# Orders of work on VectorE, ScalarE and the load queue in a two-block fp32 network, changed in six places

## What is computed

```python
h = rms_norm(x, norm1_g);  p = h @ w_in                       # 1024 -> 3328
uv = gelu(p[..., :1024]);  s_in = p[..., 1024:1280]
gates = sigmoid(p[..., 1280:] + b_gate)                        # g_a, g_b
br_a = gmlp_spatial_gating(uv[..., :512], uv[..., 512:], ...)  # layer norm of v, per group w_s @ v, times u
br_b = s5_mixer(s_in, ...)                                     # complex scan in both directions, gelu, y * sigmoid(y @ w_glu)
x = x + (g_a * (br_a @ w_up_a) + g_b * (br_b @ w_up_b)) @ w_out
x = x + expert_choice_ffn(rms_norm(x, norm2_g), ...)           # softmax, top 64 of 512 for each of 16 experts
x = rms_norm(x, final_g)
# second block
u = rms_norm_2(x);  x_lru, g_lru, q, k, v, g_ret = split(u @ w_in_2)
mixed = concat(rms_norm_2(rg_lru(conv(x_lru)) * gelu(g_lru)), group_norm(retention(q, k, v)) * silu(g_ret))
h = x + mixed @ w_out_2
up = conv(rms_norm_2(h) @ ffn_up_w);  a, v = split(up)
return rms_norm_2(h + (gelu(a) * v) @ ffn_down_w)
```

## Time and profile before

| | us |
|---|---|
| median of 3 runs (lowest to highest) | 1932.91 (1932.58 to 1933.05) |
| profiled execution, own time | 1933.91 |
| its span, first to last instruction | 1932.1 |
| PE busy | 1750.1 (91%) |
| DVE busy | 667.9 (35%) |
| ACT busy | 443.6 (23%) |

### The profile page before, as it was taken

The page is one execution under the profiler, slowest core; times in us unless marked ns, Lnnn a source line. Parts: engine busy times, 40 slices in busy tenths (PEclk is TensorE's granted clock), DMA queues, the critical chain, the costliest instruction groups (busy, mean ns, idle before and its releaser), DMA issues. The chain is left out here.

```text
span 1932.1 us, 19429 instructions
## 1 busy us (share of the span) xinstructions
PE 1750.1 (91%) x8120; PEld 1045.2 (54%) x8120; DVE 667.9 (35%) x903; ACT 443.6 (23%) x546; POOL 0.2 (0%) x4
## 2 busy tenths in 40 slices
PE   5998997899998898988979889789999999999997
PEld 4877774434342332423324233247767778888885
DVE  6865463201011010100101001047735466555644
ACT  4433322101010000100001010055433343323332
POOL 0000000000000000000000000000000000000000
PEclk9999999899999999999999999999999999999999
DMA  4313644699999999999999999950412213232311
GB/s 160 99 48 107 218 136 184 261 428 428 427 428 429 429 428 429 428 429 428 428 428 429 428 428 428 428 220 28 153 44 88 87 66 109 87 109 87 109 44 44
DMA packets 76389, 492.47 MB, mean 255 GB/s; under 512 B 7472, under 2 KB 12592, under 8 KB 51504
## 3 DMA queue, kind: packets, MB, share of 16 engines
q1 hardware_dynamic: 76336, 491.71, 63.1%
HBM read 487.49 MB, written 2.10 MB: 253 GB/s over the span
## 5 line engine op out<-in xcount | busy, mean ns | idle before, releaser
L1166 PE MATMUL ps<-xs,xe 128*64 128x512 f32 x2048 | 462.9, 600 | 65.8 <-DMA xs<-w_up 33.2
L1166 PEld LDWEIGHTS ps<-xs,xe 128*64 128x64 f32 x2048 | 142.1, 137 | 379.2 <-issue 265.9
L1178 PE MATMUL ps<-xs,hidT 128*64 128x512 f32 x1024 | 229.7, 596 | 13.6 <-DMA xs<-w_down 8.9
L412 DVE TENSOR_TENSOR lo<-raw,hi 128x2048 fp32r<-128x2048 f32 (+1 forms) x73 | 164.9, 2259 | 217.7 <-ACT hi L403 210.6
L1394 DVE TENSOR_TENSOR hid<-hid,ps 128x512 f32<-128x512 f32 x32 | 20.6, 684 | 524.3 <-PE ps L1166 524.3
L403 ACT ACTIVATE hi<-raw 128x2048 fp32r<-128x2048 f32 (+1 forms) x73 | 137.9, 1889 | 232.0 <-PE ps L466 96.9
L466 PE MATMUL ps<-xh,hi 128*128 128x512 f32 x416 | 167.8, 403 | 10.3 <-DVE ga L921 5.8
L466 PE MATMUL ps<-xl,hi 128*128 128x512 f32 x416 | 164.3, 395 | 0.0
L442 PE MATMUL ps<-xh,hi 128*128 128x512 f32 x384 | 151.4, 394 | 4.3 <-ACT hi L403 3.2
L1178 PEld LDWEIGHTS ps<-xs,hidT 128*64 128x64 f32 x1024 | 74.0, 137 | 147.6 <-issue 127.7
L442 PE MATMUL ps<-xl,hi 128*128 128x512 f32 x384 | 150.2, 391 | 0.0
(11 more groups left out here) (415 smaller groups left out, 1783.6 us busy)
## 6 DMA issues: line engine op xcount, KB each, us to landing
xs<-w_up SPq DMA_DIRECT2D x64, 2048.0 KB, 32.8
xs<-w_gate SPq DMA_DIRECT2D x64, 2048.0 KB, 31.9
xs<-w_down SPq DMA_DIRECT2D x64, 2048.0 KB, 31.3
raw<-w_in SPq DMA_DIRECT2D x25, 1024.0 KB, 7.2
raw<-ffn_up_w SPq DMA_DIRECT2D x24, 1024.0 KB, 5.1
raw<-ffn_down_w SPq DMA_DIRECT2D x12, 1024.0 KB, 5.1
raw<-w_out SPq DMA_DIRECT2D x8, 1024.0 KB, 5.1
xin<-x_t SPq DMA_DIRECT2D x4, 512.0 KB, 7.4
```

Source lines behind the costliest of these rows:

```text
L412: dve.tensor_tensor(lo[slot][:, 0:size], raw[:, raw_slot(n), 0:size], hi[slot][:, 0:size].bitcast(F32), ALU.subtract).then_inc(sem("lo_don ...
L1166: mm = pe.matmul(ps[64 * half:64 * half + 64, bank + b, :], xe[:, k, CAP * u:CAP * (u + 1)], xs[n % NXS][:, f:f + 512], start=(k == 0), st ...
L1178: mm = pe.matmul(ps[64 * nn:64 * nn + 64, YB, :], hidT[:, 4 * (c % 2) + kk, CAP * half:CAP * (half + 1)], xs[n % NXS][:, kk * D + nn * 512 ...
```

## The change

The number of matmuls, activations, vector instructions and DMAs stays; they come in another order. `prm` gets a semaphore of its own, `prm_in`. `x` and chunk 0 are issued right behind it. ACT's Exp and Sin stand before `xh`; hi and lo of chunk 0 stand in the middle of the 8 tiles. lo of 6 and the layer norm stand before `WT`, lo of 7 behind `hs_ready`. Chunk 9 is loaded before the 32 `INT` DMAs. `z` is computed for banks 2, 3, 0, 1, and only the last two wait for `yblk`. The gated unit stands behind the first quarter of chunk 12's hi part. The merges and the lo of 14 to 17 alternate. hi of 20 comes before `take_turned`. hi and lo of NEXP+1 come later, in ACT's list between tiles 3 and 4 of the second block and in DVE's behind the splits, which now follow the takes at a distance of five. hi of NFFN+5 comes between `ca` and `cv`.

```diff
+        ZQ = (2, 3, 0, 1)
...
             pe.wait_ge(sem("gm_in"), 64)
-            pe.wait_ge(sem("yblk_done"), 2)
-            for q in range(4):
+            for q in ZQ:
+                if q == 0:
+                    pe.wait_ge(sem("yblk_done"), 2)
...
-            pe.wait_ge(sem("yT_done"), 2)
-            pe.wait_ge(sem("glu_in"), 16)
-            for m in range(2):
-                for k in range(2):
-                    mm = pe.matmul(ps[:, PP + 2 + m, :], wglu[:, k, m * P:(m + 1) * P], yT[:, k, :],
-                                   start=(k == 0), stop=(k == 1))
-            mm.then_inc(sem("glu_ps"), 1)
-            chunk_mms(pe, 12, QQ, 4, 4, xh, xl, opens=False)
+            def glu():
...
+            chunk_mms(pe, 12, QQ, 4, 4, xh, xl, opens=False, after={(0, 0): glu})
...
-            act.wait_ge(sem("cst_in"), 32)
+            act.wait_ge(sem("prm_in"), 16)
             a(TY[:, 2, :], prm[:, P_DT:P_DT + SG], ACT.Exp).then_inc(sem("dt_done"), 1)
-            for k in range(KD):
-                act.wait_ge(sem(f"x_in{k // 2}"), 16)
-                a(xh[:, k, :], xin[:, k, :], ACT.Copy, scale=gains[:, 0, k:k + 1]).then_inc(sem("xh_done"), 1)
-            make_hi(act, 0)
             act.wait_ge(sem("ang_done"), 1)
...
+            for k in range(KD):
+                if k == 4:
+                    make_hi(act, 0)
+                act.wait_ge(sem(f"x_in{k // 2}"), 16)
+                a(xh[:, k, :], xin[:, k, :], ACT.Copy, scale=gains[:, 0, k:k + 1]).then_inc(sem("xh_done"), 1)
...
+            for k in range(KD):
+                if k == 4:
+                    make_lo(dve, 0)
+                rest(k)
             dve.wait_ge(sem("s5_in"), 32)
...
-            dve.wait_ge(sem("v_ps"), 4)
-            dve.tensor_copy(WT[:, 0, :, 0], y(28))
...
             make_lo(dve, 6)
-
             dve.wait_ge(sem("gm_in"), 32)
...
                 tt(vg[:, t, :], vg[:, t, :], lnv[:, 1, :], ALU.add).then_inc(sem("vn_done"), 1)
-            make_lo(dve, 7)
-
+            dve.wait_ge(sem("v_ps"), 4)
+            dve.tensor_copy(WT[:, 0, :, 0], y(28))
...
+            dve.wait_ge(sem("cst_in"), 16)
             dve.wait_ge(sem("hs_done"), 4)
...
             dve.sem_inc(sem("hs_ready"), 1)
+            make_lo(dve, 7)
             dve.memset(RD[:, :, 0:1], 0.0)
...
-            for q in range(4):
-                dve.wait_ge(sem("z_ps"), q + 1)
+            for j, q in enumerate(ZQ):
+                dve.wait_ge(sem("z_ps"), j + 1)
...
+            take(gb[1], 13)
             make_lo(dve, 14)
-            take(gb[1], 13)
-            make_lo(dve, 15)
-            make_lo(dve, 16)
-            for h in range(2):
-                dve.wait_ge(sem("pe_used"), 14 + 2 * h)
...
+            def merge(h, branch, bank, n, name, gate):
+
+                dve.wait_ge(sem("pe_used"), n)
+                dve.wait_ge(sem(gate), 4 + 4 * h)
                 for m in range(4):
-                    tt(ga[h][:, m, :], ga[h][:, m, :], ps[:, PP + m, :], ALU.mult).then_inc(sem("mrg_a"), 1)
...
+                    tt(branch[h][:, m, :], branch[h][:, m, :], ps[:, bank + m, :], ALU.mult).then_inc(sem(name), 1)
...
+            merge(0, ga, PP, 14, "mrg_a", "ga_done")
+            make_lo(dve, 15)
+            merge(0, gb, QQ, 15, "mrg_b", "gb_done")
+            make_lo(dve, 16)
+            merged(0)
+            merge(1, ga, PP, 16, "mrg_a", "ga_done")
+            make_lo(dve, 17)
+            merge(1, gb, QQ, 17, "mrg_b", "gb_done")
+            merged(1)
             make_lo(dve, 18)
...
                 square(k)
+            make_hi(act, 20)
             for t in range(NT):
                 take_turned(t, 0)
-            make_hi(act, 20)
...
                         act.wait_ge(sem("xs_used"), NX - 4)
-                        for j in range(2):
-                            make_hi(act, NEXP + j)
+                        make_hi(act, NEXP)
...
-            for j in range(2):
-                make_lo(dve, NEXP + j)
+            make_lo(dve, NEXP)
             stt = dve.scalar_tensor_tensor
-            for m in range(KD + 1):
+            for m in range(KD + 5):
                 if m < KD:
                     take_scattered(m, KD * (NE // 2) + m + 1)
-                if m:
-                    dve.wait_ge(sem("xh_done"), KD + m)
...
+                k = m - 5
+                if k >= 0:
+                    dve.wait_ge(sem("xh_done"), KD + k + 1)
...
+            make_lo(dve, NEXP + 1)
...
             for m in range(KD):
+                if m == 4:
+                    make_hi(act, NEXP + 1)
                 act.wait_ge(sem("sc_taken"), SCS - KD + m + 1)
...
                 for b in range(2):
+                    if b == 1 and not down:
+                        make_hi(act, n + 5)
                     act.wait_ge(sem("fy_done"), lin(j, i, 2, b + 1))
...
-                    elif b == 1:
-                        make_hi(act, n + 5)
...
-            d(prm[:], w["small"]).then_inc(sem("cst_in"), 16)
-            d(cst[:], w["consts"][:, 0:NSMALL]).then_inc(sem("cst_in"), 16)
-            d(BS[:].rearrange("p r g h -> p r (g h)"), w["s5b"]).then_inc(sem("s5_in"), 16)
+            d(prm[:], w["small"]).then_inc(sem("prm_in"), 16)
             for q in range(4):
                 d(xin[:, 2 * q:2 * q + 2, :], w["x_t"][:, 2 * q:2 * q + 2, :]).then_inc(sem(f"x_in{q}"), 16)
-                if q == 2:
+                if q == 1:
                     load_chunk(sp, 0)
+            d(BS[:].rearrange("p r g h -> p r (g h)"), w["s5b"]).then_inc(sem("s5_in"), 16)
+            d(cst[:], w["consts"][:, 0:NSMALL]).then_inc(sem("cst_in"), 16)
...
             d(wsT[:], w["gmlp_ws_t"]).then_inc(sem("gm_in"), 16)
+            load_chunk(sp, 9)
             sp.wait_ge(sem("hs_ready"), 1)
...
-            for n in range(9, 11):
-                load_chunk(sp, n)
+            load_chunk(sp, 10)
```

More of the change, by code:

```diff
@@ L599, in tables @@
                 mm.then_inc(sem("h_ps"), 1)
-            pe.wait_ge(sem("cst_in"), 32)
             pe.wait_ge(sem("hi_done"), 1)
@@ L613, in first_pe @@
             mm.then_inc(sem("pe_used"), 1)
+            pe.wait_ge(sem("cst_in"), 16)
             norm_sums(pe, 0, QQ + 3)
@@ L683, in first_pe @@
             mm.then_inc(sem("yT_ps"), 1)
-            pe.wait_ge(sem("yT_done"), 2)
-            pe.wait_ge(sem("glu_in"), 16)
-            for m in range(2):
-                for k in range(2):
-                    mm = pe.matmul(ps[:, PP + 2 + m, :], wglu[:, k, m * P:(m + 1) * P], yT[:, k, :],
-                                   start=(k == 0), stop=(k == 1))
-            mm.then_inc(sem("glu_ps"), 1)
-            chunk_mms(pe, 12, QQ, 4, 4, xh, xl, opens=False)
+            def glu():
+                pe.wait_ge(sem("yT_done"), 2)
+                pe.wait_ge(sem("glu_in"), 16)
+                for m in range(2):
+                    for k in range(2):
+                        mm = pe.matmul(ps[:, PP + 2 + m, :], wglu[:, k, m * P:(m + 1) * P], yT[:, k, :],
+                                       start=(k == 0), stop=(k == 1))
+                mm.then_inc(sem("glu_ps"), 1)
+            chunk_mms(pe, 12, QQ, 4, 4, xh, xl, opens=False, after={(0, 0): glu})
             pe.wait_ge(sem("sg_done"), 2)
@@ L794, in first_act @@
             make_hi(act, 12)
-            for m in range(4):
-                act.wait_ge(sem("uz_done"), m + 1)
+            for j, m in enumerate(ZQ):
+                act.wait_ge(sem("uz_done"), j + 1)
                 a(bah[:, m, :], uT[:, m, :], ACT.Copy).then_inc(sem("bah_done"), 1)
@@ L837, in first_dve @@
             dve.memset(eps, EPS).then_inc(sem("eps_done"), 1)
-            dve.wait_ge(sem("cst_in"), 32)
+            dve.wait_ge(sem("prm_in"), 16)
             y = lambda i: prm[:, P_LRE + SG * i:P_LRE + SG * i + SG] if i < 2 else TY[:, i, :]
@@ L850, in first_dve, with rest @@
             ts(y(7), y(7), -1.0, HALF_PI, ALU.mult, ALU.add).then_inc(sem("ang_done"), 1)
-            for k in range(KD):
+            def rest(k):
                 dve.wait_ge(sem("xh_done"), k + 1)
@@ L854, in first_dve @@
                     .then_inc(sem("xl_done"), 1)
-            make_lo(dve, 0)
             dve.wait_ge(sem("exp_done"), 4)
@@ L967, in first_dve @@
                 tt(vg[:, t, :], vg[:, t, :], lnv[:, 1, :], ALU.add).then_inc(sem("vn_done"), 1)
-            make_lo(dve, 7)
+            dve.wait_ge(sem("v_ps"), 4)
+            dve.tensor_copy(WT[:, 0, :, 0], y(28))
+            L(dve.tensor_copy(WT[:, 1, :, 0], y(29)))
+            for m in (1, 2, 4, 8, 16, 32):
+                tm = [TMP[:, r, 0:SG * m].rearrange("p (g k) -> p g k", g=SG) for r in range(2)]
+                cmul([WT[:, r, :, m:2 * m] for r in range(2)], [WT[:, r, :, 0:m] for r in range(2)],
+                     [WT[:, r, :, m - 1:m].to_broadcast([P, SG, m]) for r in range(2)], tm)
+            dve.wait_ge(sem("cst_in"), 16)
             dve.wait_ge(sem("hs_done"), 4)
@@ L1006, in first_dve @@
             dve.wait_ge(sem("u_tok"), 1)
```

(27 more changed lines are left out.)

2 lines of the change are left out of this document (1 added, 1 removed).

## The result

| us | before | after |
|---|---|---|
| median (lowest to highest) | 1932.78 (1932.58 to 1933.05), 4 runs | 1888.34 (1888.28 to 1889.88), 4 runs |
| profiled execution, own time | 1933.91 | 1889.88 |
| its span | 1932.1 | 1888.1 |
| PE busy | 1750.1 | 1737.5 |

The ratio is 0.977, its 95% interval 0.9758 to 0.9782. The forecast was 1890.2 in a range of 1884 to 1903.

A forecast was written before the change was run, and what follows sets the result against it. The prediction took the experts to go at the weight stream's pace, 427 GB/s, and PE to lose time in waits and low clock elsewhere. Its terms summed to 42.7 us, 1932.9 - 42.7 = 1890.2 us, range 1884 to 1903.

The forecast's parts named there:

- A: Start: chunk 0 lands earlier and PE begins near 15.6 instead of 20.9 us; 4.7 us gained, bounds 3 to 7.
- B1: Chunks 6 to 9: the wait at chunk 6, most of that at chunk 9 and their low clock go; 14.8 us.
- DVE becomes the bound: Rival: in chunks 6 to 9 scans, lo of 9 and take come 7 us later; 1897.7 us, chance 0.08.
- B2: z and the gated unit: the waits of 0.8 us for `yblk` and 1.4 for `yT` go; 2.2 us.
- C: Merges: two waits of PE, 4.9 and 1.3 us, and 1.6 us of low clock go; 7.8 us.
- D: Routing: with hi of 20 earlier, 3.1 us of wait and 1.8 us of low clock go; 4.9 us.
- F: Feed-forward, part 0: waits of 0.5 and 2.7 us and 1.6 us of low clock go; 4.8 us.
- the clock falls anyway: Rival: the waits go but the low clock stretches, 11.1 us in all, stay; 1901.3 us, chance 0.05.
- E: Last expert: `yy` starts 2.65 us earlier, PE idles 2.5 us instead of 5.1; 3.5 us with 0.9 of clock.
- The gain stops at the experts: Rival: the weight stream sets the end of the experts, so only the gains behind them are left; 1924.6 us, chance 0.05.
- Slower: Rival: the experts' weight stream loses rate; gain gone at 407.5 GB/s, 1951 us at 400; chance 0.03.
- Doesn't do what it says: Rival: another wait ends last at each place, only the start and small waits gain, about 7 us; 1926 us, chance 0.02.

The follow-up runs named there:

- fill_start: The kernel after with 20 added matmuls on the parameters, results unread, ahead of the first real matmul; 1887.23 us.
- fill_tail: The kernel after with 5 added matmuls, results unread, ahead of PE's wait for `yy` behind the last expert; 1889.64 us.
- old_load9: The kernel after with chunk 9 loaded behind the 32 `INT` DMAs again, DVE's order as changed; 1892.08 us.
- all_fills: The kernel after with 20 added matmuls at the start, lo of N2+12 behind `ml`, and fills at `htk`, `idm`, `s` and `yy`; 1882.39 us.

## Why the prediction was right, point by point

**Start (A), 4.7 forecast, 5.25 measured.** Chunk 0 was forecast to land at 11.2 and hi to end at 13.1. ACT in order of time, answering to the earlier trace rows:

```profile
10.99 1.91 ACT L403 ACTIVATE hi<-raw 128x2048 fp32r<-128x2048 f32 x1 [1.25 <-DMA raw<-w_in]
```

It landed at 10.97, and PE began at 15.3 instead of 15.6. The 0.6 us given back for the clock at the start were too much here: 5.6 of lead fell to 5.25, that is 0.35. This part is luck either way, since the low clock behind the first matmul cost 1.4 to 2.7 us in the traces without a fill.

The prediction said that no row shows the order of completion, and gave 9.4 for chunk 0 by ordered completion, without a working. The earlier trace rows do show two landings in the order of issue, chunk 0 at 13.8 and the last part of x at 15.2, and its own 11.2 supposes that order. In the kernel after the loads landed as issued: x at 5.83 and 8.05, chunk 0 at 10.97, x at 12.25 and 13.54, `BS` at 13.84. It isn't strict: in fill_start `BS`, issued last of these, landed at 13.48 and the part of x before it at 13.88.

**Chunks 6 to 9 (B1), 14.8 and 14.9.** The steps were worked out on the times of before, so 5.25 are to be taken off them. DVE in order of time, answering to the earlier trace rows:

```profile
102.91 0.18 DVE L971 COPY WT<-TY 128x16 f32<-128x16 f32 x1
...
114.32 2.29 DVE L412 TENSOR_TENSOR lo<-raw,hi 128x2048 fp32r<-128x2048 f32 x1 [0.23 <-DVE HS L983]
...
117.25 2.48 DVE L931 TENSOR_TENSOR gb<-ps,rb 128x512 f32<-128x512 f32 x4
...
134.25 4.47 DVE L996 TENSOR_TENSOR_SCAN T<-RD,Zs 128x1024 f32<-128x1024 f32 x2
138.75 2.29 DVE L412 TENSOR_TENSOR lo<-raw,hi 128x2048 fp32r<-128x2048 f32 x1
141.89 2.48 DVE L931 TENSOR_TENSOR ga<-ps,rb 128x512 f32<-128x512 f32 x4 [0.84 <-PE ps L466]
```

`WT` was forecast for 108.2 - 5.25 = 102.95, the end of the first quarter of take(`gb[0]`) for 117.85 (it begins at 117.25 and takes 0.69), the end of the scans for 138.95 (138.72); PE reached chunk 7 at 119.80 (120.15 forecast). lo of 9 ends at 141.0, PE's last matmul of chunk 8 at 141.85, and PE waits for the take's first quarter: 0.78 us, forecast 0.8. SP's `INT` run behind the load of chunk 9 until 138.1 (145 - 5.25 = 139.8 forecast), and PE waits for nothing that hangs on them:

```profile
117.05 21.07 SPq L2073 DMA_DIRECT2D INT<-HS  x32
```

So "DVE becomes the bound" fell: DVE stood idle for 0.84 us ahead of the take, waiting for PE.

**B2, C, D, F: 19.7 forecast, 21.2 measured.** All waits named went. What is left over is 0.1 to 0.5 us each, and it is the same thing: a wait costs more than its idle time in the row. Before the change, at 1582 us:

```profile
1582.35 0.79 PE L442 MATMUL ps<-xh,hi 128*128 128x512 f32 x1 [2.71 <-ACT hi L403]
1582.94 0.63 PE L442 MATMUL ps<-xl,hi 128*128 128x512 f32 x1
1583.36 0.63 PE L442 MATMUL ps<-xh,hi 128*128 128x512 f32 x1
```

The matmul before it began at 1579.25, so 3.10 us lie between two starts that are 0.23 apart without a wait: 2.87 lost, 0.16 more than the 2.71 of the row, since each matmul is shown 0.16 us longer than the distance to the next start (its end is modelled). And the first one behind takes 0.59 to the next start, those after it 0.43: 0.16 more. The lead grows by 2.88 us at this wait and by another 1.57 over the low clock behind it; the 1.6 forecast for that was measured from the first matmul on, so it has the second 0.16 in it, but not the first. Where the clock stayed up, both are missing: the waits of 0.8, 1.4, 1.3 and 0.5 us were worth 1.1, 1.7, 1.6 and 0.7. The step of the prediction that was short is "a wait costs more than itself": it had the clock in it, not these 0.16 us at three of the seven waits and 0.3 at the other four, which is about the 1.5 us.

**Routing, experts: -1.3 and +0.5, forecast 0.** This loss was not seen. PE's windows of the same instructions, before, then after:

```profile
326.56:330.00 3.44, 1.70 (x16) 1.00 1.06 452
343.60:349.90 6.30, 4.88 (x23) 0.50 0.02 4
```

```profile
290.50:294.59 4.09, 2.95 (x16) 0.50 1.04 445
308.76:314.40 5.64, 4.22 (x19) 0.50 0.02 4
```

The order and the waits here are the same (1.5 us for `htk`, 14.2 for `idm`). Before, the 16 matmuls between the two waits ran at full clock in 1.70 us; after, at 0.50 in 2.95. The low clock behind the long wait is in both. The prediction cited, from the Trainium skill (TensorE: Matmul & The Clock Gate, section What's actually happening), that the moment of the switch is free-running and differs between runs. This case agrees: fill_tail and fill_start, with the same instructions here, have it fall only inside the long wait, and each gains 1.2 us on the kernel after over these 16 matmuls and the few around them. Of the 13 traces in which this wait of 1.5 us for `htk` stands, the clock fell at it in seven, so it was luck that it held in the trace before and not in the one after; without that the lead would be 45.3 and not 44.0. It changed the sum by 1.3 us, not by the 11.1 of the rival "the clock falls anyway": where the waits of the earlier trace rows went, the clock held. (The prediction calls that rival its third; it is the second of its list.)

**Last expert (E), 3.5 forecast, 3.4 measured.** ACT in order of time, answering to the earlier trace rows:

```profile
1232.67 1.91 ACT L403 ACTIVATE hi<-raw 128x2048 fp32r<-128x2048 f32 x1 [15.97 <-DMA raw<-w_in]
1234.61 1.39 ACT L1304 ACTIVATE yy<-ps,cur 64x512 f32<-64x512 f32 x2
```

`yy` follows one hi instead of two, 2.64 us of wait went, and 0.8 us of clock, estimated as 0.9. The second figure is partly luck: the clock fell behind the 2.5 us left in ten of eleven traces, and not in old_load9.

**The other rivals.** "The gain stops at the experts": a lead of 35.1 us entered and 35.3 left. "Slower": 427 GB/s in both, 895 and 894 us. "Doesn't do what it says": the table of leads has each step at its place. One sum of the chances is off: all but the last rival and half of the fourth is 0.96, not 0.95.

What stays open: which of the waits of 1.3 to 2.5 us will lower the clock in a given run. The 0.8 us at chunk 9 did in none of these traces, the 1.8 for `kr` in three of 14, the 1.5 for `htk` in seven of 13, the 2.5 for `yy` in ten of 11. Length alone doesn't decide: in the first expert (336.8 us in the kernel after) PE stands for 1.32 us between dense matmuls, and in 13 of 14 traces the clock is low for 3.4 us behind it, while it held behind the 1.34 and 1.45 us that the kernel before has at the second merge and at `yT`. So the prediction was right that the 0.8 us for `yblk` and the 1.4 for `yT` brought no low clock, but 1.4 us is not too short for one. No run here tells beforehand.

## What to carry to other kernels

On an engine that runs a list in order, ask of each instruction ahead of a wait who needs it, and when: moving the ones that nobody waits for yet (a rounding, a table, 32 small DMAs ahead of one large load) gave 44 us here with not one instruction less. Work out the new order instruction by instruction from measured durations until the next wait appears; that held to 0.4 us for the engines in the stretch of chunks 6 to 9 (the small DMAs ended 1.7 us earlier than worked out). Count each removed wait as its idle time, plus some 0.3 us of drain and restart, or 0.16 where the low clock behind it is counted from the first matmul on, plus that low clock. Expect the clock to take or give one or two us at another short wait, and don't read a change of that size from a single span.

## What the runs showed of the hardware

- Of the fills of waits, only the one at the start shows a gain that stays: 2.1 and 2.45 us over the kernel after by the starts of the matmuls. The fill at `yy` won 1.6 us and lost 1.6 at the next short wait, in both kernels that had it. The 24 ahead of `idm` ended 2.1 us too early and gained nothing; 29 with their neighbours gained 2.0 us of span at most, of which 1.2 may be chance.
- The clock fell behind 1.5 us of idle PE that followed 12.8 us of uninterrupted matmuls (all_fills, 306.7 us), and behind 1.32 us in the first expert (kernel after: 10 matmuls begin in the 3.5 us from 338.2, at a granted clock of 0.51).
- Behind the waits of 2.5 us for `yy` and 1.8 for `kr` the low clock lasted 3.4 us and cost 1.5 to 1.7 us, where two of the kernels can be compared.
- The load queue's order at the start is worth 2.7 us for 0.95 MB moved behind chunk 0; 0.37 MB/us, read from two landings before, gave 2.6. Eleven traces with the new order of loads have chunk 0 landing between 10.2 and 11.3.
